# Two differential heads' mixes issued together, gaps in the operands' buffers, and transposes behind the next heavy item

## What is computed

```python
def diff_attention(q, k, v, lam, lam_init, subln_g):
    scale = q.shape[-1] ** -0.5
    def block(qb):
        logits = jnp.einsum('bqhmd,bthmd->bhmqt', qb, k).astype(jnp.float32) * scale
        p = jax.nn.softmax(logits, axis=-1)
        w = p[:, :, 0] - lam * p[:, :, 1]
        return jnp.einsum('bhqt,bthd->bqhd', w.astype(v.dtype), v)
    o = sweep_query_blocks(block, q)
    return rms_norm_2(o, subln_g) * (1.0 - lam_init)

def gla_chunk_scan(q, k, v, logf, s0):
    """S_t = diag(f_t) S_{t-1} + k_t^T v_t ; o_t = q_t S_t, in chunks of HG_CHUNK."""
...
        bcum = jnp.cumsum(fc, axis=1)
        o_inter = jnp.einsum('bthk,bhkv->bthv', qf * jnp.exp(bcum), s)
        diff = bcum[:, :, None] - bcum[:, None, :]
        decay = jnp.exp(jnp.where(incl[None, :, :, None, None], diff, -jnp.inf))
        att = jnp.einsum('bthk,bshk,btshk->bhts', qf, kf, decay)
        o_intra = jnp.einsum('bhts,bshv->bthv', att, vf)
```

## Time and profile before

| | us |
|---|---|
| median of three runs | 1472.39 |
| lowest and highest | 1470.36, 1472.88 |
| profiled execution | 1471.23 |
| its span in the trace | 1469.5 |

### The profile page before, as it was taken

One profiled execution on the slowest core, in us unless ns is written; L12 is line 12 of the kernel. 1 busy time (PEld: TensorE's weight loads), 2 busy tenths in 40 slices (PEclk: granted clock), 3 DMA queues, 4 the chain that ended last, 5 costly groups with the idle time before them and its releaser, 6 DMA issues.

```text
span 1469.5 us, 20226 instructions
## 1 busy us (share of the span) xinstructions
PE 1411.3 (96%) x8130; PEld 1155.2 (79%) x8130; DVE 563.9 (38%) x1335; ACT 415.0 (28%) x771; POOL 157.2 (11%) x191
## 2 busy tenths in 40 slices
PE   5999999999999999999999999999979999999986
PEld 3888788888878888888888888877757788887765
DVE  1262322111226432313235431245664533466363
ACT  2112212412011222333323312331333422433432
POOL 0110300000011030000111100003230000142100
PEclk9999999999999999999999999999989999999998
DMA  9544544355445444443333332455313433322200
GB/s 388 218 163 152 206 172 172 134 200 194 184 164 211 175 173 172 149 179 117 141 126 132 115 127 103 144 200 201 116 58 144 172 119 147 126 112 87 87 29 29
DMA packets 31485, 221.76 MB, mean 151 GB/s; under 512 B 3872, under 2 KB 4000, under 8 KB 4896
## 3 DMA queue, kind: packets, MB, share of 16 engines
q1 hardware_dynamic: 31392, 220.47, 40.5%
HBM read 219.41 MB, written 1.05 MB: 150 GB/s over the span
## 4 chain that ended last, share of the span: by engine, by line
PE 84%; DVE 7%; ACT 2%; issue 2%; POOL 2%; DMA 1%; DVEq 0%; SPq 0%; ACTq 0%; POOLq 0%
PE event L879 43%; PE event L870 9%; PE event L1023 6%; PE event L1067 5%; PE logits L955 3%; PE mixed_out L1011 3%; PE event L836 3%; PE event L1035 2%; PE turns L974 2%; PE event L1167 2%; PE event L1094 1%; DMA ring<-in_w 1%; PE event L1048 1%; DVE logits L1612 1%; ACT S L1284 1%
## 5 line engine op out<-in xcount | busy, mean ns | idle before, releaser
L879 PE MATMUL event<-u,ring 128*128 128x256 f32 x3200 | 717.7, 383 | 15.3 <-ACT region L1233 9.5
L879 PEld LDWEIGHTS event<-u,ring 128*128 128x128 f32 x3200 | 605.7, 191 | 113.0 <-issue 30.9
L870 PE MATMUL event<-ring,u 128*128 128x256 f32 (+1 forms) x704 | 150.9, 371 | 0.0
L870 PEld LDWEIGHTS event<-ring,u 128*128 128x128 f32 x704 | 127.4, 190 | 20.9 <-issue 4.9
L1975 POOL TENSOR_TENSOR raw<-raw,tables 128x512 f32<-128x512 f32 (+1 forms) x28 | 44.7, 1595 | 758.3 <-DVE turned L1588 449.5
L1248 ACT ACTIVATE region<-event 128x512 f32<-128x512 f32 x72 | 43.0, 597 | 279.9 <-PE event L879 279.7
L1284 ACT ACTIVATE S<-logits,stat 128x512 f32<-128x512 f32 (+2 forms) x160 | 83.8, 535 | 127.8 <-DVE stat L1627 123.2
L1067 PE MATMUL event<-region,ring 128*128 128x256 f32 x384 | 85.1, 380 | 2.9 <-DVE region L1770 2.9
L1023 PE MATMUL event<-region,ring 128*128 128x256 f32 x384 | 84.4, 380 | 0.0
L1067 PEld LDWEIGHTS event<-region,ring 128*128 128x128 f32 x384 | 72.2, 190 | 15.2 <-issue 5.9
L1023 PEld LDWEIGHTS event<-region,ring 128*128 128x128 f32 x384 | 72.6, 190 | 11.1 <-issue 1.4
(11 more groups left out here) (208 smaller groups left out, 1307.5 us busy)
## 6 DMA issues: line engine op xcount, KB each, us to landing
ring<-in_w SPq DMA_DIRECT2D x204, 1024.0 KB, 4.8
tables<-in_two SPq DMA_DIRECT2D x1, 1472.0 KB, 8.0
x<-in_x SPq DMA_DIRECT2D x1, 1024.0 KB, 14.8
x<-in_ctx SPq DMA_DIRECT2D x1, 1024.0 KB, 6.7
out<-x SPq DMA_DIRECT2D x4, 256.0 KB, 2.2
tables<-in_one SPq DMA_DIRECT2D x1, 768.0 KB, 9.9
tables<-in_late SPq DMA_DIRECT2D x1, 512.0 KB, 5.6
consts<-in_common SPq DMA_DIRECT2D x1, 320.0 KB, 3.3
```

Source lines behind the costliest of these rows:

```text
L870: ins = mm(bank[:, t * 256:t * 256 + width], mem.u[:, q, k, t * P:(t + 1) * P], wt[:, k * 256:k * 256 + width], start=k == 0, stop=k == KB ...
L879: ins = mm(bank[:, j * 256:(j + 1) * 256], wt[:, k * 256 + j * P:k * 256 + j * P + P], mem.u[:, q, k, :], start=k == 0, stop=k == KB - 1)
```

## The change

There are three parts.

1. `joined` names the even jobs among a latent section's differential ones. `weave` leaves out their `mix`; the odd job's `mix` does both, one matmul for each head in turn for each tile of keys, and DVE copies both halves at once.
2. `modulate` puts the `ada` behind the next heavy item after its `mva` pair, where it was two items behind.
3. The buffer of gaps is no longer used for the scan's preps. POOL writes gap p into the operands' buffer p mod 2, ACT and DVE work in place. So POOL waits for PE to have read what that buffer held, the level two preps back (`readers`), and no more for DVE's product p-1.

```diff
+def one_head(job):
+
+    return job.kind == "F" and len(job.maps) == 2
+
+
+def joined(jobs):
+
+    return [n for n, job in enumerate(jobs) if one_head(job) and n % 2 == 0]
...
-def weave(jobs, fill):
+def weave(jobs, fill, joined=()):
...
-        if n >= 2:
+        if n >= 2 and n - 2 not in joined:
             s.append(("mix", n - 2))
...
-def modulate(s, at, lag, groups):
+def modulate(s, at, groups):
+
+    after = {a: min(n for n in heavy(s) if n > a) for a in at}
     out = []
     for n, item in enumerate(s):
         out.append(item)
+        for (tag, g), a in zip(groups, at):
+            if after[a] == n:
+                out.append(("ada", g, tag))
         for (tag, g), a in zip(groups, at):
             if a == n:
                 out += group(tag, g)
-            if a + lag == n:
-                out.append(("ada", g, tag))
...
+    def event(self, item):
+
+        e, seen = self.phase, []
+        for i in self.script:
+            i = i[1] if i[0] == "half" else i
+            if i == item:
+                return e
+            if i not in seen:
+                e += self.events(i)
+                seen.append(i)
+
+    def readers(self, s, m):
+
+        if m == "khat":
+            e = self.event(("khatT", s))
+            return [e, e + 1]
+        if m == "qc":
+            return [self.event(("hout", s))]
+        e = self.event(("level", s, m))
+        return [e, e + 1]
...
             elif kind == "mix":
                 n, job = item[1], sec.jobs[item[1]]
+                first = n - 1 if one_head(job) else n
                 eng.wait_ge(sems["turns_copied"], w.at("turns_copied", n + 1))
-                eng.wait_ge(sems["y_copied"], w.at("y_copied", n))
+                eng.wait_ge(sems["y_copied"], w.at("y_copied", first))
...
-                if job.kind == "C":
+                if one_head(job):
+                    for kt in range(job.keys // P):
+                        for j in (first, n):
+                            (m, s, _), = heads_of(sec.jobs[j])
+                            ins = mm(mem.out[HD * s:HD * s + HD, 0:P], value_of(mem, sec.jobs[j], m, kt),
+                                     mem.PT[:, j % 2, kt * P:(kt + 1) * P], start=kt == 0, stop=kt == job.keys // P - 1)
+                elif job.kind == "C":
...
-                ins.then_inc(sems["mixed"], 1)
+                ins.then_inc(sems["mixed"], n + 1 - first)
...
-                act(mem.gaps, mem.gaps, ACT.Exp).then_inc(sems["decays_ready"], 1)
+                act(ops, ops, ACT.Exp).then_inc(sems["decays_ready"], 1)
...
-                    tt(ops[:, 0], gaps[:, 0], to["hq"], ALU.mult)
+                    tt(ops[:, 0], ops[:, 0], to["hq"], ALU.mult)
...
-                at = preps.index((s, m))
-                eng.wait_ge(sems["ops_ready"], w.at("ops_ready", at))
-                gaps, FG = mem.gaps, mem.of[s, layer_of(sec, s)]["FG"]
+                p = preps.index((s, m))
+                if p >= 2:
+                    for ev in sec.readers(*preps[p - 2]):
+                        eng.wait_ge(full[ev % BANKS], w.fills(ev))
+                gaps, FG = mem.ops[:, p % 2], mem.of[s, layer_of(sec, s)]["FG"]
```

More of the change, by code:

```diff
@@ L198, in script_one0 @@
     groups = [("w0", 4), ("w0", 5)] + [("w1", g) for g in range(6)]
-    s = modulate(s, heavy(s)[3::5][:8], 2, groups)
+    s = modulate(s, heavy(s)[3::5][:8], groups)
     s.insert(s.index(("ada", 5, "w1")) + 1, ("cond",))
@@ L239, in script_one1 @@
         fill[min(at + h, len(fill) - 1)] += items
-    s += weave(len(jobs), fill) + [i for f in fill for i in f]
-    s = modulate(s, heavy(s)[2::4][:6], 2, [("v0", g) for g in range(6)])
+    s += weave(len(jobs), fill, joined(jobs)) + [i for f in fill for i in f]
+    s = modulate(s, heavy(s)[2::4][:6], [("v0", g) for g in range(6)])
     n = s.index(("ada", 3, "v0")) + 1
@@ L307, in script_two0 @@
         fill[h + 1].append(("ada", g, "v1"))
-    s += weave(len(jobs), fill)
+    s += weave(len(jobs), fill, joined(jobs))
     s += [("sq", "f0"), ("half", ("outa", 3, (0,))), ("norm", "f0"), ("outa", 3, (0,)), ("gate", 0, 1), proj("vv", 1), ("outb", (0,))]
@@ L328, in script_two1 @@
     fill[n].insert(0, ("norm", "h0"))
-    s += weave(len(jobs), fill) + [("sq", "f0"), ("half", ("outa", 3, (0,))), ("norm", "f0"), ("outa", 3, (0,)), ("gate", 0, 1)]
+    s += weave(len(jobs), fill, joined(jobs)) + [("sq", "f0"), ("half", ("outa", 3, (0,))), ("norm", "f0"), ("outa", 3, (0,)), ("gate", 0, 1)]
     return s + [("outb", (0,)), ("mean", 0), ("var", 0), ("affine", 0, 1)]
@@ L984, in body @@
                         eng.wait_ge(drained[ev % BANKS], w.fills(ev))
-                elif n == 0 or sec.jobs[n - 1].kind != job.kind and job.kind != "N":
+                elif first == 0 or sec.jobs[first - 1].kind != job.kind and job.kind != "N":
                     ev = arrival(w, "fv" if job.kind == "F" else "vv", 0, job.seq)
@@ L1186, in body @@
         sqs = [i[1] for i in sec.script if i[0] == "sq"]
-        preps = [i[1:] for i in sec.script if i[0] == "prep" and i[2] != 0]
+        all_preps = [i[1:] for i in sec.script if i[0] == "prep"]
+        preps = [p for p in all_preps if p[1] != 0]
         stick = 0
@@ L1677, in body @@
                 y = mem.one["y"] if job.kind in "ABC" else mem.of[job.seq, job.layer]["y"]
-                sides = {s for _, s, _ in heads_of(job)}
-                rows = slice(0, P) if len(sides) == 2 else slice(HD * min(sides), HD * min(sides) + HD)
                 nb = max(b for _, _, b in heads_of(job)) + 1
@@ L1683, in body @@
                 else:
[L1684 to L1686 removed]
+                    dst = y[:, base + b0:base + b0 + nb, qt * P:(qt + 1) * P]
+                    src = mem.out[:, 0:nb * P].rearrange("p (b t) -> p b t", t=P)
+                eng.tensor_copy(dst, src).then_inc(sems["y_copied"], 2 if one_head(job) else 1)
                 eng.wait_ge(sems["y_copied"], w.at("y_copied", n + 1))
```

21 lines of the change are left out of this document (7 added, 14 removed).

## The result

The changed kernel is slower. Its median of eleven runs is 1475.52 us (1472.63 to 1478.09), against 1470.97 us for the kernel before (1469.81 to 1472.88, eleven runs beside it). The ratio is 1.0027, 95% interval 1.0018 to 1.0036, so about +4 us. Measured once more it was 1.0021 (1.0013 to 1.0030). I had said 1467, with a range of 1463 to 1472 and a chance of 0.11 for slower.

A forecast was written before the change was run, and what follows sets the result against it. PE was taken as the bound, busy 96%. Joined mixes in two0 -4.1, two1 -2.5, transposes -0.3, gaps +2.1 gave -4.8 us: 1466.4 from the profiled run, 1467.6 from the median, stated as 1467, range 1463 to 1472.

The forecast's parts named there:

- Joined mixes, PE time: Latent sections: two differential jobs' mixes overlap as one of 1.02 us, removing 4.1 us of PE work in each section.
- PE has no idle time in that window, so I take the whole: two0, second half (1100 to 1213 us): PE fully busy, so the whole 4.1 us of removed mixes is gained.
- The tail of two1: Last differential jobs of two1: PE waits on a DVE and ACT chain; three copies and an earlier last turn shorten it.
- together 2.5 us in two1: two1's tail: 1.1 us from three vanished DVE copies plus 1.4 us from an earlier last turn; between 1.5 and 4.1.
- the gain is what leaves that chain: two1's tail: only time leaving the DVE and ACT chain that PE waits for counts as gain, 2.5 us.
- The gaps: Scan preps in the operands' buffers: POOL's later waits delay ACT and DVE, +2.1 us in sum, bounds -1 to +7.
- the +0.4: two0, PE's wait at 1033.67: POOL's next gap falls on DVE's small softmax operations, up to +0.9 us, taken as 0.4.
- the feed starts 0.95 us late: two0's scan: a 2.3 us slip is partly recovered through the gap at 1077.86, so PE at 1092.94 is +0.95 us.
- half is made up by 1328: two1's scan: exponential slips 3.3 us, half recovered by DVE operations no longer meeting POOL; +0.75 us left at 1351.45.
- each scan step has whole projections around it as cover: one1: PE's projections around every scan step hide the late gaps, so +0 us.
- Rival (a): Slower: late gaps hold ACT and DVE at all 16 latent steps; 0.43 us each cancels the gain, half price 1488; chance 0.11.
- The transposes: `ada` behind the next heavy item: one0's 0.88 us wait goes, 0.6 us returns before its output projection; net -0.3 us.

The follow-up runs named there:

- the best kernel: Kernel before plus the transposes' part and joined mixes, except jobs 8 and 9 of two1; gaps in their own buffer: ratio 0.9967, median 1467.08 us.
- the filled kernel: Changed kernel plus unused matmuls on PE in three idle places of two1's tail (nine, five, two): ratio 0.9993 to the kernel before, median 1471.56 us.
- version with three buffers: Changed kernel with three operands' buffers for two, gap p waiting for the level three steps back: ratio 0.9998 to the kernel before, median 1470.61 us.
- the gaps' kernel: Kernel before with only the gaps written into the operands' buffers: ratio 1.0044, median 1477.35 us.
- the joined kernel: Kernel before with only the joined mixes: ratio 0.9975, median 1468.42 us.
- filling only the first idle place: Changed kernel plus nine unused matmuls in the 3.10 us idle time ahead of two1's first output projection: ratio 1.0022 to the kernel before, median 1475.44 us.

## Why the prediction was wrong

**Joined mixes, PE time: right.** Sixteen records in 1.09 us, 4.3 us for the section. In two0 3.25 us arrived and not 4.1 (3.47 in the best kernel). The step that failed there is "PE has no idle time in that window, so I take the whole": taking a mix away made a wait of 0.80 us, which didn't exist, ahead of the output projection at 1184.19. The window was full because the mix stood in it.

**The tail of two1: the mechanism was right, and it missed a price.** The step "together 2.5 us in two1" gives what the filled kernel shows, 2.57. But I looked at what the removed mixes did for the chain and not at what they did for the clock. Mix 8 stood between two waits of 0.84 and 1.37 us. Without it PE is idle for 3.10 us at a stretch, and in the three profiles of the changed kernel and its version with three buffers the clock then fell to 1.2 GHz for the whole projection: 5.46 - 2.83 = 2.6 us, 0.3 to 0.4 on the mix behind it, and at the last jobs, behind idle times of 1.34 and 0.77 us, another 1.6. That is 4.6 us, and -2.5 became +2.05. So the step that failed is "the gain is what leaves that chain": it put what PE's own speed does in the longer idle time at nothing, without a reason. No rival of mine had the clock. The profile held the hint: at 1092.94 the projection follows 9.54 us of idle time, and the window from 1088 to 1098 has a granted clock of 0.60:

```profile
1088.00:1098.00 10.00, 5.06 (x17) 0.60 0.00 0
```

The Trainium skill says it outright ("TensorE: Matmul & The Clock Gate", Part 1: The HAM clock gate): the gate is throttled by default, and activity releases it. The traces agree: 0.60 in this window, 0.66 in that of the changed kernel.

**The gaps: the mechanism was right, three sizes were off.** The places in two0 and two1 are where the replay had them, one1's I had put at nothing, and the wait for the level is the whole cost. The terms were +0.95 and +0.4 in two0 (measured +1.33 and +0.06), +0.75 in two1 (+2.72) and 0 in one1 (+1.46). In two0 the +0.4 was right where I had it: the wait at 1033.67 went from 1.20 to 1.67 us, and 0.39 came back at 1011.47, where a wait for DVE fell from 1.65 to 1.25. The failed step is "the feed starts 0.95 us late". It starts 2.04 us late, since the gap that I had set free now falls on DVE's two products, 1.59 us in place of 0.75 (the row at 1083.55). With PE at full speed that arrives whole, +2.04 in the gaps' kernel. In the changed kernel PE's slow records push POOL's next gap back, the feed runs 3.98 us in place of 4.69, and +1.33 is left: luck. In two1 the step that failed is "half is made up by 1328". The exponential slipped by 3.5 us, where I had 3.3: it stands 4.29 us behind the level's start and stood 0.79 behind. But only 0.8 us of it was made up, and 2.72 arrived: 0.40 at the new wait, the rest where 0.27 us became 2.63. Two softmax operations that no longer meet POOL (0.62 and 0.47 us before, 0.16 and 0.17 now) are worth those 0.8 us. The two products at 1323.20 do meet it and take 1.61 us in place of 0.75, and behind them the softmax, the exponentials and the products follow each other on DVE and ACT. In one1 the failed step is "each scan step has whole projections around it as cover". One gap has a merge behind it, and a merge is no cover: its sigmoid is queued on ACT behind the late exponential. I had looked at PE's work around the step and not at what was queued behind it on ACT.

**Rival (a)** had the right place and sign: it decided from 0.43 us in each of the 16 latent steps, and these cost 4.1 us, 0.26 a step, with 1.5 more in one1. By itself that leaves a forecast of -1.3 us, or -0.4 with what two0's join fell short; slower came out only with the clock's 4.6 us on top. **The transposes** were small, as said: -0.3 predicted, -0.9 measured with an interval that takes in both. By the rows the changed kernel has -0.87 in one0 and +0.49 in one1, where I had nothing, -0.4 together.

**What is open.** The parts alone add up to -3.7 + 6.5 - 0.9 = +1.9 us, and the whole costs +3 to +4. The interval of each is 1.5 us to either side, so this may be nothing; or the joined kernel meets the low clock more often when the other parts are there (5.46 us against 4.44). Late gaps are not needed for that: the kernel with three buffers has none and shows 5.46 us and a slow last mix too. With one or two profiles for each kernel that can't be told. Nor is it shown why filling only the first idle place gained nothing on average, so what each of the two slow stretches costs on average is open: the 4.6 us are those of single profiles, and the ratios show 4.1 for both together.

## What to carry to other kernels

Work that stands between two waits of TensorE may cost nothing where it lies, and removing it may cost the clock: before taking work out, look at what idle time is left in one piece, not only at whether the engine's busy time falls. When a buffer is given up, ask what its old wait kept apart and what its new wait waits for; "written in place" is free, and a wait for a reader one step back is not. And cover is to be counted on every engine in whose queue the late instruction stands.

## What the hardware showed that I had not expected

- 3.10 us of idle time were followed by the low clock in each of the four profiles that had it: twelve records took 5.46 us in three and 4.44 in one (2.83 at full clock). With the idle time filled down to 0.9 us they took 2.83 in both kernels that did so.
- It doesn't need one piece that long. Behind 2.37 us of idle time in two0's scan the next sixteen records took 4.92 to 5.21 us in five of seven profiles, and 3.72 in two. And behind 1.34 and 0.77 us of idle time, with a 0.66 us turn between them, the last mix took 1.88 to 1.97 us in four profiles, and 1.09 in four others with the same waits.
- Extra matmuls of 4.3 us made a kernel 2.5 to 4.1 us faster.
- Two products of 128x256 on DVE took 0.76 us alone and 1.58 to 1.61 us with POOL's subtractions beside them, at three places. A removed wait of POOL for DVE had kept them apart.
